# Splitting the first layer's cross values and probabilities into rounded parts, on a one-core Trainium2 kernel of two hybrid layers

## What is computed

```python
def _cross_attention(h, mem, norm_g, norm_m, w_q, w_kv, qn, kn, w_out):
    u = _rmsnorm(h, norm_g)
    mn = _rmsnorm(mem, norm_m)
    q = _rmsnorm((u @ w_q).reshape(b, s, CROSS_HEADS, CROSS_DIM), qn)
    kv = mn @ w_kv
    k = _rmsnorm(kv[..., :d].reshape(b, m, CROSS_HEADS, CROSS_DIM), kn)
    v = kv[..., d:].reshape(b, m, CROSS_HEADS, CROSS_DIM)
    sc = jnp.einsum('bshd,bmhd->bhsm', q, k).astype(jnp.float32) * (CROSS_DIM ** -0.5)
    pr = jax.nn.softmax(sc, axis=-1).astype(v.dtype)
    o = jnp.einsum('bhsm,bmhd->bshd', pr, v).reshape(b, s, d)
    return o @ w_out
```

## Time and profile before

| | |
|---|---|
| median of the runs | 995.97 us |
| the profiled execution's own time | 995.02 us |
| its span, first to last instruction | 993.2 us |
| TensorE busy | 838.5 us (84%) |
| VectorE busy | 466.9 us (47%) |
| ScalarE busy | 334.3 us (34%) |
| DMA | 294.73 MB, 297 GB/s on the mean |
| mean granted TensorE clock | 0.932 |

### The profile page before, as it was taken

How to read it: one execution, slowest core, us unless ns; L and a number is a source line. 1 busy time by engine, 2 the same in 40 slices (tenths; PEclk the granted TensorE clock), 3 DMA queues, 4 the chain that set the end, 5 groups by cost and what they waited for, 6 DMA issues and landing times.

```text
span 993.2 us, 13272 instructions
## 1 busy us (share of the span) xinstructions
PE 838.5 (84%) x5377; PEld 587.3 (59%) x5377; DVE 466.9 (47%) x922; ACT 334.3 (34%) x560; POOL 23.4 (2%) x35
## 2 busy tenths in 40 slices
PE   9999999999976665758466585757999999999997
PEld 8788888898631221313122131312887899999996
DVE  5788767764521120302003030201867788565695
ACT  5766745854110000101010010001434655555533
POOL 1021010100000000000000000000000000000000
PEclk9999999999997887978778887979999999999999
DMA  8753566597999999999999999999555445353531
GB/s 314 271 170 127 171 245 220 201 400 274 382 434 426 438 420 437 428 428 436 428 430 431 432 431 427 426 436 394 197 170 172 147 149 168 130 171 127 187 133 63
DMA packets 57724, 294.73 MB, mean 297 GB/s; under 512 B 3938, under 2 KB 4676, under 8 KB 49220
## 3 DMA queue, kind: packets, MB, share of 16 engines
q1 hardware_dynamic: 56212, 290.91, 74.6%
q10 hardware_dynamic: 1456, 3.03, 0.8%
HBM read 292.88 MB, written 1.05 MB: 296 GB/s over the span
## 4 chain that ended last, share of the span: by engine, by line
PE 59%; DMA 35%; ACT 2%; DVE 2%; SPq 1%; issue 1%; POOL 0%; POOLq 0%; ACTq 0%; DVEq 0%
PE bank L2601 13%; PE bank L2603 12%; PE bank L2602 12%; DMA uT<-in_down_units 12%; DMA uT<-in_up_units 10%; DMA uT<-in_gate_units 10%; PE bank L3038 5%; PE bank L2535 3%; PE bank L3061 3%; DMA ring<-in_gate_units 2%; DMA ring<-in_first_blocks 2%; PE bank L3152 1%; PE bank L3356 1%; PE bank L2797 1%; ACT ring_rounded L984 1%
## 5 line engine op out<-in xcount | busy, mean ns | idle before, releaser
L1531 DVE TENSOR_TENSOR ring_rounded<-ring,ring_rounded 128x2048 fp32r<-128x2048 f32 x76 | 174.2, 2292 | 103.9 <-ACT ring_rounded L984 103.6
L984 ACT ACTIVATE ring_rounded<-ring 128x2048 fp32r<-128x2048 f32 x75 | 143.5, 1914 | 156.8 <-PE bank L2603 142.4
L3038 PE MATMUL bank<-ring,main 128*32 128x512 f32 x760 | 105.8, 703 | 62.6 <-DMA ring<-in_up_units 44.6
L2602 PE MATMUL bank<-ring_rounded 128*128 128x256 f32 (+1 forms) x448 | 140.3, 313 | 0.0
L2603 PE MATMUL bank<-ring_rounded 128*128 128x512 f32 x320 | 124.9, 390 | 0.0
L3038 PEld LDWEIGHTS bank<-ring,main 128*32 128x32 f32 x760 | 27.4, 126 | 134.0 <-issue 111.5
L2601 PE MATMUL bank<-uT_rounded,ring_rounded 128*128 128x256 f32 x320 | 92.6, 289 | 0.0
L2603 PE MATMUL bank<-uT_rounded,ring_rounded 128*128 128x256 f32 x320 | 90.5, 283 | 0.0
L2602 PEld LDWEIGHTS bank<-ring_rounded 128*128 128x128 f32 x448 | 85.4, 191 | 4.8
L2601 PE MATMUL bank<-ring_rounded,uT_rounded 128*128 128x512 f32 x208 | 82.9, 398 | 0.5 <-DVE ring_rounded L1531 0.3
L2602 PE MATMUL bank<-ring_rounded,uT_rounded 128*128 128x512 f32 x208 | 81.0, 390 | 0.0
(11 more groups left out here) (365 smaller groups left out, 1393.1 us busy)
## 6 DMA issues: line engine op xcount, KB each, us to landing
ring<-in_up_units SPq DMA_DIRECT2D x11, 4096.0 KB, 33.4
ring<-in_w_in SPq DMA_DIRECT2D x42, 1024.0 KB, 5.0
ring<-in_down_units SPq DMA_DIRECT2D x10, 4096.0 KB, 31.9
ring<-in_gate_units SPq DMA_DIRECT2D x9, 4096.0 KB, 33.4
main<-in_gate_units SPq DMA_DIRECT2D x4, 3072.0 KB, 30.3
main<-in_down_units SPq DMA_DIRECT2D x3, 3072.0 KB, 32.7
main<-in_up_units SPq DMA_DIRECT2D x3, 3072.0 KB, 30.3
ring<-in_w_ckv SPq DMA_DIRECT2D x8, 1024.0 KB, 5.1
```

What stands on the lines that cost most here:

```text
L984: a.activation(rounded(hi_half(name, h)), raw_half(name, h), ACT.Copy).then_inc(hi_made, 1)
L1531: v.tensor_tensor(rounded(raw), raw, as_f32(hi_half(name, h)), ALU.subtract).then_inc(split_made, 1)
L2602: mm(dst, left[0], right[1], start=False, stop=False, skip_group_check=True)
L3038: last = mm(bank[2 + part][on, :], xg3[:, h * (KC // 2) + k, on], expert_piece(j, p, u, e, KC)[:, k, :], start=h + k == 0, stop=h * (KC // ...
```

## The change

The values `cv` are split once, ahead of the heads. ScalarE writes the high part of each of the two tiles (128x1024) into `cv_hi`, the rounded twin of `normed`; VectorE subtracts it in place. The turned probabilities of each head are split too: `c_turned` on ScalarE writes the high part and counts in `hi_moved`, the new `probs_lo` on VectorE writes the low part into one of two new tiles `c_pT_lo` and drains the bank. TensorE forms three products of rounded parts for each one of before, 48 in all, and waits in front of each head for both value tiles. Since `c_pT_lo` takes `main[:, 5376:6400]` and `cv_hi` lives in `normed`, the loads of staged piece 3 (1 MB) and of the first half of staged piece 0 (0.5 MB) are issued behind the last head, ahead of block `xv2`.

In ScalarE's list the first half of `co0` is split behind the turned heads 0 and 1 and no longer ahead of them.

```diff
--- before.py
+++ after.py
@@ -173,7 +173,7 @@
 HI_BANKS = [f"{x}T{c}" for x in ("x", "mem") for c in range(4)] + [f"mixT{c}" for c in (2, 3, 0, 1)]
 HI_BANKS += [f"{x}T{c}" for x in ("ck", "h1") for c in range(4)]
 HI_BANKS += [f"{x}T{c}" for half in (0, 2) for x in ("mem2", "cq") for c in (half, half + 1)]
-HI_BANKS += [f"co_{c}" for c in range(4)] + [f"h3T{c}" for c in range(4)]
+HI_BANKS += ["cpT0", "cpT1", "co_0", "cpT2", "co_1", "cpT3", "co_2", "co_3"] + [f"h3T{c}" for c in range(4)]
 HI_BANKS += [f"n3T{c}" for c in range(4)]
 ROPED = ["iq", "ik", "dq2", "dk2", "mq", "mk"]
 RELUS = ["il0_0", "il0_1", "il1_0", "il1_1", "il1_2", "il1_3"]
@@ -338,6 +338,7 @@
         mem2_lo = c.take(2048)
         c_prob += [c.take(512)]
         c_pT = [c.take(512) for _ in range(2)]
+        c_pT_lo = [c.take(512) for _ in range(2)]
         c.at = 6400
         cq_tok, cqT = c.take(2048), c.take(2048)
         mem2_rows, mem2_spread = main[:, 1536:1536 + T], main[:, 4864:4864 + T]
@@ -349,6 +350,7 @@
         ckT, cv = c.take(2048), c.take(2048)
 
 
+        cv_hi = normed[:, :, :].rearrange("p t d -> p (t d)")
         lo_a, lo_b = ring[:, 3 * SLOT:3 * SLOT + 2048], ring[:, 3 * SLOT + 2048:4 * SLOT]
         coT = lo_b
 
@@ -442,6 +444,7 @@
         router_scaled, router_args = sem("router_weights_scaled"), sem("router_exponents_ready")
         router_exp = sem("router_exp")
         index_query_hi = sem("first_half_of_index_queries_hi_made")
+        values_hi, values_split = sem("cross_values_hi_made"), sem("cross_values_split")
         index_hi, index_split = sem("index_weights_hi_made"), sem("index_weights_split")
         after_experts, merged = sem("after_experts"), sem("merged")
         summed, merged_hi = sem("branches_summed"), sem("merged_hi_made")
@@ -734,6 +737,8 @@
                     wait_filled(sp, "co_3")
                     load_piece(0, GROUP - 1, gate_w)
                     load_staged(2, [0])
+                    load_staged(0, [0])
+                    load_staged(3)
                 load_dense(name)
                 if name == "cq0":
                     wait_filled(sp, "mixT1")
@@ -745,12 +750,11 @@
                     load_piece(2, 2, up_w)
                     load_staged(2, [1])
                     sp.wait_ge(head_summed, len(HEAD_SQUARES))
-                    load_staged(0)
+                    load_staged(0, [1])
                     wait_filled(sp, "cs1_1")
                     load_piece(2, 0, up_w)
                     load_piece(0, 2, gate_w)
                     load_piece(2, 1, up_w)
-                    load_staged(3)
 
             def load_part(b, e, units, k):
 
@@ -1233,7 +1237,8 @@
             def c_turned(hh):
                 if hh >= 2:
                     wait_filled(act, f"co_{hh - 2}")
-                copy(f"cpT{hh}", c_pT[hh % 2])
+                src = wait_filled(act, f"cpT{hh}")
+                a.activation(rounded(c_pT[hh % 2]), src[:, :], ACT.Copy).then_inc(hi_moved, 1)
 
             def co_hi(hh):
                 hi_of(f"co_{hh}", coT[:, hh * 512:(hh + 1) * 512])
@@ -1241,9 +1246,14 @@
             c_exps(0)
             split_hi("xk2", [1])
             c_exps(1)
-            split_hi("co0", [0])
+            for t in range(TT):
+                wait_drained(act, f"cv0_{t}")
+                wait_drained(act, f"cv1_{t}")
+                at = slice(t * D, (t + 1) * D)
+                a.activation(rounded(cv_hi[:, at]), cv[:, at], ACT.Copy).then_inc(values_hi, 1)
             c_turned(0)
             c_turned(1)
+            split_hi("co0", [0])
             split_hi("co0", [1])
             co_hi(0)
             c_turned(2)
@@ -2002,6 +2012,18 @@
             pair_bias("c", 3, c_neg(3))
             pair_weights("c", 2, c_prob)
             pair_weights("c", 3, c_prob)
+            for t in range(TT):
+                dve.wait_ge(values_hi, t + 1)
+                at = slice(t * D, (t + 1) * D)
+                v.tensor_tensor(rounded(cv[:, at]), cv[:, at], as_f32(cv_hi[:, at]), ALU.subtract)\
+                    .then_inc(values_split, 1)
+
+            def probs_lo(hh):
+
+                lo_of(f"cpT{hh}", c_pT_lo[hh % 2], c_pT[hh % 2])
+
+            for hh in (0, 1):
+                probs_lo(hh)
             split_lo("co0", [0])
             wait_drained(dve, "mrow1")
             for half in range(2):
@@ -2012,6 +2034,8 @@
             for hh in range(4):
                 at = slice(hh * 512, hh * 512 + 512)
                 lo_of(f"co_{hh}", lo_a[:, at], coT[:, at])
+                if hh < 2:
+                    probs_lo(hh + 2)
             NG, NE = N_GROUPS, N_EXPERTS
             dve.wait_ge(params_landed, 16 * N_PARAMS)
             at = COLS["norm_ffn"][0]
@@ -2936,11 +2960,15 @@
                     c_turn(hh + 1)
                 b = wait_free(f"co_{hh}")
                 wait_drained(pe, f"cpT{hh}")
+                pe.wait_ge(values_split, TT)
+                v_hi, v_lo = (as_tiles(rounded(x)) for x in (cv_hi, cv))
+                p_hi, p_lo = rounded(c_pT[hh % 2]), rounded(c_pT_lo[hh % 2])
                 for c in range(2):
                     for kt in range(TT):
-                        lo = hh * CROSS_D + c * P
-                        last = mm(b[:, c * T:(c + 1) * T], cv3[:, kt, lo:lo + P],
-                                  c_pT[hh % 2][:, kt * T:(kt + 1) * T], start=kt == 0, stop=kt == 1)
+                        at, keys = slice(hh * CROSS_D + c * P, hh * CROSS_D + c * P + P), slice(kt * T, (kt + 1) * T)
+                        for part, (x, p) in enumerate(((v_hi, p_hi), (v_hi, p_lo), (v_lo, p_hi))):
+                            last = mm(b[:, c * T:(c + 1) * T], x[:, kt, at], p[:, keys], start=kt + part == 0,
+                                      stop=kt == 1 and part == 2)
                 full(f"co_{hh}", last)
 
             def out_halves(h):
```

## The result

The changed kernel takes 1000.03 us, the median of 6 runs (998.50 to 1000.98); the kernel before took 995.70 in as many (995.03 to 996.29). The ratio is 1.0043 with a 95% interval of 1.0033 to 1.0053: slower by 4.3 us. A second set of runs gave 999.74 against 995.46, 1.0042 (1.0029 to 1.0056). The profiled execution took 999.91.

What follows compares the result with a forecast made beforehand. TensorE products bound the two layers, expert-weight transfers the middle; the change lies on TensorE's path. Stall +2.5, clock +1.0 and transfers 0 gave +3.5 us on 995.02, so 998.5, or 999.5 on the runs' median; range 996.2 to 1001.6.

Steps and rivals of the forecast that it cites:

- The sum: Whole kernel: +2.5 for the stall, +1.0 for the clock and 0 for transfers make +3.5 us.
- wait on the values: Ahead of head 0: TensorE's wait for the value splits, costed at nothing, 0.5 us at most.
- second wait: At head 3: none expected, as its subtraction ends 1.2 us after head 2's, whose products take 1.4 us.
- four passes: Heads' products: the skill's rule, three passes in place of four, would save 1.7 us; the forecast took 1.3.
- Stall term: Ahead of head 2: TensorE idle 3.8 us behind VectorE's list, less 1.3 saved on products, +2.5 us (2.1 to 3.1).
- Clock term: Behind the gap at head 2: a fall of TensorE's granted clock, +1.0 us, ends 0 and +2.15.
- rival 2: At head 2: the stall with the full clock fall, +2.5 + 2.15 us, 1000.6; chance 0.18.
- dense work on both sides: Around the gap at head 2: argument for a stall without a clock fall, +2.5 us, 998.5; chance 0.22.
- Transfers: Loads moved behind the last head: 1.5 MB, 3.5 us of DMA time, fit the hole in 230 to 240 us; 0.
- Delay passed on: From co0 to the end: a delay of TensorE reaches the expert stream and the kernel's end one for one.
- rival 3: Before 254.5 us: the expert stream swallows the delay, so not slower, 996.0 to 997; chance 0.13.
- Releaser: At head 2: TensorE's gap is released by VectorE's subtraction into main_rounded, not by ScalarE.

Runs made afterwards that it cites:

- filled gap: The changed kernel with 14 idle 128x128 products put on TensorE ahead of its wait for head 2: 997.86 us against 995.55 for the kernel before, 1.0025.
- middle gap: The changed kernel with co0's second-half low part made behind the heads, plus a 128x1024 VectorE step ahead of co_0's low part: 997.90 us against 995.46, 1.0022.
- run with two products: The changed kernel without the low part of the probabilities, 32 products, turned banks drained by ScalarE: 995.33 us against 995.46 for the kernel before, 1.0002.
- run with one step moved: The changed kernel with VectorE making the low part of co0's second half behind head 3's low part: 995.45 us against 995.55 for the kernel before, 1.0001.

## Why the prediction was right

**The sum.** The forecast difference was +3.5 us and the measured one +4.3. The mechanism, a stall of TensorE behind VectorE's list with a fall of the clock behind it, is the one that the runs show; the size of the clock term was too small. That 999.5 came within 0.5 us of 1000.03 is in part luck: the kernel before had a median of 995.97 in the forecast's three runs and of 995.70 in six, which hid 0.3 us of the miss.

**Head by head.** "Head 2's subtraction ends at about 219.6": it ended at 220.34 in an execution that was 0.82 late from its start, 219.5. The idle 3.8 us were 3.65. The wait on the values cost nothing (head 0 started straight behind xk2), and no second wait came at head 3. The products took 117 ns, but the 24 of heads 2 and 3 took 3.08 us at full clock where 2.8 was forecast, so that 5.9 us and not 5.6 stand against the 6.92: 1.0 us saved. The 1.7 us by the four passes of the Trainium skill (FP8 and Floating Point Precision, TensorE Precision Notes) would have been further off. "Co0 starting 2.1 to 3.1 us later" was missed, with 4.0: the clock fell in the midst of the heads' products, which stand ahead of co0. The 219.88 us for co0's start before added up two views; the row stands at 219.68.

**Stall term, +2.5.** The filled gap shows 2.3 us by the runs and 2.7 by trace.

**Clock term, +1.0: mis-sized.** It was the one open term, and I took it below its nearest row. It measured 1.5 us by trace and 2.0 by the runs. The row itself was read short: the window behind the 4.00 us gap ended at 379.5 us, but the clock stayed at half until 380.4. The chain of the kernel before has the price in full, the same 32 products behind that gap and behind one without a fall:

```profile
376.12 5.38 PE bank L3038 x32
...
415.08 3.69 PE bank L3038 x32
```

The difference is 1.7 us where the prediction took 1.2 from the row and 1.0 into the sum. The lower end was read short as well: the window of 1.2 us is part of an idle stretch of 2.03 us (354.74 to 356.77), behind which the clock stayed at 1.00. The full fall of rival 2, at 2.15, was too much by trace; its 1000.6 missed the median by 0.6 us, the forecast by 0.5. The Trainium skill (TensorE: Matmul & The Clock Gate, Part 1) has the throttled clock as the default that activity lifts. The filled gap agrees, with 1.00 all through it; but the fall was not as sure as the prediction had it by that rule, since 1.47 us had none. The argument that dense work on both sides might spare the clock was wrong: in the middle gap eight runs of eleven paid, by their times.

**Transfers, 0.** Shown by the run with the loads alone, to the 0.9 us or so of its interval and, up to co0, by its trace. The hole in 230 to 240 us was filled as described.

**Delay passed on.** 4.2 us at the first transfer of the chain and 4.3 at the end: rival 3, the stream swallowing the delay, falls, although the DMA engines' last holes before it were partly filled.

**Releaser.** I expected the profile to name VectorE. It gave "issue"; only the end time in VectorE's timeline, and the runs that moved or lengthened a step of it, show the cause.

## What to carry to other kernels

When work is moved from the busiest engine to one with 47% busy time, read the other engine's list at that place, instruction by instruction, and ask what stands ahead of the step that is newly waited for; here a 2.2 us weight split stood there that TensorE needs only for co0's second half, 5.5 us behind co0's start. Order such a list by due time, and check the next block too, since the wait may only move. Here a gap in TensorE of 2.7 us and more cost more than its length in most runs, so one that can't be removed may be worth filling. And when a term is taken from a row, follow the row until its effect ends.

## What the runs showed of the hardware

- A gap of 1.47 us in dense work cost nothing beyond its length. In the profiled executions 2.72 us cost 1.5 us more, 3.65 us 1.5 us (2.0 by the runs' medians) and 6.01 us 2.4 us. By their times three of eleven runs with the gap of 2.72 us paid nothing more. In the run with two products a gap of 1.86 us at co0, with a wait of 0.55 us some 4 us ahead of it, was followed by a fall in the profiled execution as well.
- The length alone doesn't decide. In the expert phase of the kernel before, six gaps of 2.03 to 2.54 us left the clock at 1.00 for the 5 us behind them; the one of 4.18 us that ended at 376.12 did not. The run with one step moved has two gaps there of 3.55 and 3.90 us (up to 601.58 and 669.81) without a fall behind them. What tells them apart is open.
- At half clock a product of 128x256 on the rounded type took 213 ns for 117, 1.8 times as long, so a fall of 3.41 us lost 1.5 us and not 1.7.
- 28 idle instructions of TensorE in the gap kept the clock at 1.00 and made the kernel 1.5 us faster by trace, some 2 by the medians.
- A fall may come after the gap is over: it ended at 220.44 and the clock fell at 221.9, in the midst of the products. In the kernel before the gap that ended at 376.12 was followed by one at about 377.1. Behind the gap of 6.01 us it was there already, from about 221.5.
